# RWKV-7 heads in a decoder trunk: operands loaded once for two right sides, a chunk inverse kept in one orientation, and a row load moved behind the scan

## The reference, cut to what matters

```python
def step(state, inp):
    r_t, w_t, k_t, v_t, kk_t, a_t = inp
    sa = jnp.einsum('bhvk,bhk->bhv', state, -kk_t)
    state = (state * w_t[:, :, None, :] + sa[..., None] * (kk_t * a_t)[:, :, None, :]
             + v_t[..., None] * k_t[:, :, None, :])
    return state, jnp.einsum('bhvk,bhk->bhv', state, r_t)
```

## Time and profile before

| | us |
|---|---|
| median of 3 runs (lowest, highest) | 1743.28 (1740.84, 1746.19) |
| the profiled execution, its own time | 1744.99 |
| its span, first to last instruction | 1743.3 |
| PE busy | 1661.1 (95%) |
| DVE busy | 1001.9 (57%) |
| ACT busy | 738.5 (42%) |

### The profile page before, as it was taken

The page is one execution under the profiler, slowest core; times in us unless marked ns, Lnnn a source line. Parts: engine busy times, 40 slices in busy tenths (PEclk is TensorE's granted clock), DMA queues, the critical chain, the costliest instruction groups (busy, mean ns, idle before and its releaser), DMA issues.

```text
span 1743.3 us, 26994 instructions
## 1 busy us (share of the span) xinstructions
PE 1661.1 (95%) x11106; PEld 1385.8 (79%) x11106; DVE 1001.9 (57%) x1272; ACT 738.5 (42%) x985; POOL 144.2 (8%) x160
## 2 busy tenths in 40 slices
PE   7999998999899999999999989989999999999996
PEld 5777898888778888888877767878887788888885
DVE  3578564674675543434488974555657755434346
ACT  4535543363435232323267864624543542323231
POOL 6110110000000000000016630000000000000000
PEclk9999999999999999999999999999999999999998
DMA  5221002353133333333332320243521233333331
GB/s 198 73 74 37 4 4 99 133 152 105 35 102 93 99 95 99 95 99 119 97 121 73 97 73 25 83 130 101 159 85 40 94 109 97 97 97 97 97 121 61
DMA packets 41162, 159.75 MB, mean 92 GB/s; under 512 B 4560, under 2 KB 4688, under 8 KB 39632
## 3 DMA queue, kind: packets, MB, share of 16 engines
q1 hardware_dynamic: 40752, 155.93, 28.8%
q10 hardware_dynamic: 288, 2.10, 0.3%
HBM read 153.81 MB, written 4.19 MB: 91 GB/s over the span
## 4 chain that ended last, share of the span: by engine, by line
PE 79%; DVE 13%; ACT 4%; issue 2%; DMA 1%; POOL 1%; SPq 0%; DVEq 0%; ACTq 0%; POOLq 0%
PE bank L582 23%; PE bank L584 23%; PE bank L583 23%; DVE w_lo L1772 2%; DVE act_lo L1785 1%; DVE sconv L1788 1%; DVE h L1788 1%; ACT w_hi L1255 1%; DMA w_raw<-weights 1%; PE bank L763 1%; PE bank L1104 1%; DVE stage L2172 1%; DVE bank L1788 1%; PE bank L782 1%; PE bank L776 1%
## 5 line engine op out<-in xcount | busy, mean ns | idle before, releaser
L1772 DVE TENSOR_TENSOR w_lo<-w_raw,w_hi 128x1024 fp32r<-128x1024 f32 x263 | 325.8, 1240 | 313.5 <-ACT w_hi L1255 310.7
L582 PE MATMUL bank<-act_lo,w_hi 128*128 128x512 f32 x1048 | 417.2, 398 | 27.2 <-DVE w_lo L1772 16.0
L1255 ACT ACTIVATE w_hi<-w_raw 128x1024 fp32r<-128x1024 f32 x263 | 278.8, 1061 | 350.2 <-PE bank L584 336.3
L583 PE MATMUL bank<-act_hi,w_lo 128*128 128x512 f32 x1048 | 412.4, 394 | 0.0
L584 PE MATMUL bank<-act_hi,w_hi 128*128 128x512 f32 x1048 | 412.1, 393 | 0.0
L582 PEld LDWEIGHTS bank<-act_lo,w_hi 128*128 128x128 f32 x1048 | 199.3, 190 | 75.3 <-issue 17.3
L584 PEld LDWEIGHTS bank<-act_hi,w_hi 128*128 128x128 f32 x1048 | 199.2, 190 | 42.3
L583 PEld LDWEIGHTS bank<-act_hi,w_lo 128*128 128x128 f32 x1048 | 199.3, 190 | 41.7 <-issue 1.2
L582 PE MATMUL bank<-w_lo,aux_hi 128*128 128x512 f32 x576 | 224.9, 390 | 0.0
L583 PE MATMUL bank<-w_hi,aux_lo 128*128 128x512 f32 x576 | 224.4, 390 | 0.0
L584 PE MATMUL bank<-w_hi,aux_hi 128*128 128x512 f32 x576 | 224.4, 390 | 0.0
(11 more groups left out here) (362 smaller groups left out, 2058.6 us busy)
## 6 DMA issues: line engine op xcount, KB each, us to landing
w_raw<-weights SPq DMA_DIRECT2D x263, 512.0 KB, 3.6
gb<-ln_rows SPq DMA_DIRECT2D x6, 1024.0 KB, 7.2
stage<-x_feat SPq DMA_DIRECT2D x4, 512.0 KB, 6.2
h<-x_tok SPq DMA_DIRECT2D x1, 2048.0 KB, 7.7
stage<-mem_feat ACTq DMA_DIRECT2D x2, 1024.0 KB, 6.1
spill<-h SPq DMA_DIRECT2D x1, 2048.0 KB, 7.4
h<-spill SPq DMA_DIRECT2D x1, 2048.0 KB, 7.9
out<-h SPq DMA_DIRECT2D x4, 512.0 KB, 2.6
```

Source lines behind the costliest of these rows:

```text
L582: pe.matmul(o, whi, xlo, start=first, stop=False)
L583: pe.matmul(o, wlo, xhi, start=False, stop=False)
L1255: act.activation(w_hi[:, s], w_raw[:, s], ACT.Copy).then_inc(S("w_hi_done"), 1)
L1772: dve.tensor_tensor(w_lo[:, s], w_raw[:, s], f(w_hi[:, s]), ALU.subtract).then_inc(S("w_split"), 1)
```

## The change

1. `within_chunks` makes eight tiles from 64 products instead of ten from 160: each stationary operand (nbh, kh) is loaded once for 128 moving columns, 64 of rho and 64 of alpha, by an access pattern over two places (`both`). One DVE operation masks both halves and writes them to two places. The product alpha x nbh the other way round is gone.
2. The inverse is updated in one orientation: NBH for v below 5, XT_ for v = 5. After the first step and after each level below 5 DVE transposes the 32x32 blocks of the whole tile (`dve.transpose`, 128x1024). `level_z` makes one tile instead of two. The masks of a level stand for the other triangle.
3. `transitions(b, 0)` becomes `solved(b)`, `transitions(b, 1)` becomes `transitions(b)`: 32 products of 128 columns each instead of 64 of 64. ACT writes `rgt`, and DVE adds `rat`, to two places at a time.
4. The `rw` tiles move out of `within_chunks`: group 0 behind the bonus products, group 1 behind the LRU products. `bonus(1)` on DVE moves behind a convolution, `lru_scan` one level later with scans 2 and 3 behind the levels.
5. `lru_hi(0)` and `lru_hi(1)` on ACT move into the state loop, after states 3 and 6. The load of h moves behind chunk out0+5 and the end of the scan.

Cut to what is spoken of ("..." marks what is left out):

```diff
@@ sync
-                if c == FIRST["out0"] + 2:
-                    sp.wait_ge(S("rst_mm"), 1)
+                if c == FIRST["out0"] + 5:
+                    sp.wait_ge(S("ro_mm"), 2)
                     sp.dma_start(h[:], x_tok).then_inc(S("h_moved"), 16)
@@ helper
+        def both(rows, first, second, *inner):
+            one = mix[rows, (first - h_at) // 4:(first - h_at) // 4 + 1]
+            return bass.AP(one.tensor, one.offset, [one.ap[0], ((second - first) // 4, 2), *inner])
@@ tensor: within_chunks
-                for n, (lhs, rhs) in enumerate([(alpha, nbh), (nbh, alpha), (kh, alpha), (nbh, rho), (kh, rho)]):
...
+                for n, lhs in enumerate([nbh, kh]):
+                    for j in range(2):
+                        o = [take(f"rprod{b}", 4 * n + 2 * j + q) for q in range(2)]
+                        for m in range(NT):
+                            for q in range(2):
+                                feat = slice(RD * q, RD * q + RD)
+                                for c in (2 * m, 2 * m + 1):
+                                    right = both(feat, rho_at(b, j) + c * RC * 4, alpha_at(b, j) + c * RC * 4, (1, RC))
+                                    last = pe.matmul(o[q][rows_(c), m * P:m * P + P], lhs[feat, j, c * RC:c * RC + RC],
+                                                     right, start=True, stop=True)
@@ tensor: level_z
-                x_, y_ = NBH[b], yt_(b, v)
+                y_ = yt_(b, v)
                 pe.wait_ge(*out_sem(f"ryt{b}_{v}", 1))
-                if v < 5:
...
-                o = take(f"rz{b}_{v}", 1 if v < 5 else 0)
+                if v > 1:
+                    pe.wait_ge(S("r_xt"), 2 * (v - 2) + b + 1)
+                left, right = (XT_[b], y_) if v < 5 else (y_, XT_[b])
+                o = take(f"rz{b}_{v}", 0)
@@ tensor: solved
+                                    right = both(rows_(c), act_unit(7 + 4 * b, j) + at, alpha_at(b, j) + at, (1, RC))
+                                    last = pe.matmul(o[rows_(c), (2 * m + q) * P:(2 * m + q) * P + P],
+                                                     XT_[b][rows_(c), j, ct], right, start=True, stop=True)
@@ tensor: even_mixer
                 within_chunks(0)
                 bonus(1)
+                keys_times_values(0)
                 within_chunks(1)
                 lru()
+                keys_times_values(1)
@@ scalar
-            lru_hi(0)
-            lru_hi(1)
...
+                if c == 3:
+                    act.wait_ge(S("ro_tokens"), 2)
+                    lru_hi(0)
                 if c in (4, 5):
                     group_squares(c - 4)
+                if c == 6:
+                    lru_hi(1)
@@ vector
+                masks = m_two[:].unsqueeze(2).to_broadcast([P, 2, NT, RC])
+                for n in range(8):
...
+            def first_level(b):
                 for j in range(2):
...
+                    step(tt(three(XT_[b][:, j]), three(M_[b][:, j]), mid(m_lev[:, 0], NRC), MUL))
+                    step(tt(three(XT_[b][:, j]), three(XT_[b][:, j]), mid(eye2[:], NRC), ADD))
+                done(dve.transpose(NBH[b][:], XT_[b][:]), "r_x0")
 
             masked_products(0)
-            bonus(1)
+            first_level(0)
             for j in range(2, 4):
                 dve.wait_ge(S("in_out"), 15 + j)
                 convolution(j)
+                if j == 2:
+                    bonus(1)
             masked_products(1)
+            first_level(1)
...
+                done(tt(view, view, bank(f"rz{b}_{v}", 0)[:].rearrange("p (b n) -> p b n", n=n), ADD), "rz_out")
+                if v < 5:
+                    done(dve.transpose(XT_[b][:], NBH[b][:]), "r_xt")
...
-                    if b == 0 and v >= 3:
-                        lru_scan(v - 3)
+                    if b == 0 and v >= 4:
+                        lru_scan(v - 4)
+            lru_scan(2)
             lru_scan(3)
```

More of the change, by code:

```diff
@@ L468, in _ @@
             fill(m_lev[:], 1.0)
-            for v in range(6):
+            for q in range(2):
+                rows = slice(RC * q, RC * q + RC)
+                view = m_lev[rows, 0].rearrange("p (b u) -> p b u", u=2)
+                sel(view, ALU.is_equal, 0, [[-2, RC // 2], [0, 2]], 1, 0.0)
+                sel(view, ALU.is_ge, -1, [[0, RC // 2], [1, 2]], 0, 0.0)
+            for v in range(1, 6):
                 n = 1 << v
@@ new lines, in solved @@
+            def solved(b):
+                for j in range(2):
+                    for half in range(2):
+                        o = take(f"rgt{b}", 2 * j + half)
+                        for m in (0, 1):
+                            for q in range(2):
+                                for c in (4 * half + 2 * m, 4 * half + 2 * m + 1):
+                                    ct, at = cols_(c, q), cols_(c, q).start * 4
+                                    right = both(rows_(c), act_unit(7 + 4 * b, j) + at, alpha_at(b, j) + at, (1, RC))
+                                    last = pe.matmul(o[rows_(c), (2 * m + q) * P:(2 * m + q) * P + P],
+                                                     XT_[b][rows_(c), j, ct], right, start=True, stop=True)
+                        last.then_inc(S("mixer_mm"), 1)
@@ new lines, in transitions @@
+            def transitions(b):
+                pe.wait_ge(*out_sem(f"rgt{b}", 4))
+                for j in range(2):
+                    o = [take(f"rat{b}", 2 * j + s) for s in range(2)]
+                    for m in range(NT):
+                        for c in (2 * m, 2 * m + 1):
+                            s = c % 2
+                            for q in range(2):
+                                ct, at = cols_(c, q), cols_(c, q).start * 4
+                                right = both(rows_(c), h_at + (2 * b + j) * 2048 + at, act_unit(4 * b, j) + at, (1, RC))
+                                last = pe.matmul(o[s][RD * q:RD * q + RD, m * P:m * P + P], KH[b][rows_(c), j, ct], right,
+                                                 start=True, stop=True)
+                            if m == NT - 1:
+                                last.then_inc(S("mixer_mm"), 1)
@@ L1364, in _ @@
             tokens(0)
+            values_in(0)
             tokens(1)
```

198 lines of the change are left out of this document (72 added, 126 removed).

## The result

The changed kernel takes **1726.26 us** (median of four executions, 1725.62 to 1727.52), against 1743.15 (1740.84 to 1746.19) for the kernel before, run beside it: a ratio of 0.9897, 95% interval 0.9878 to 0.9917. It is faster by 17 us, where 21.8 were forecast, and lies inside the range of 1713 to 1733. The profiled execution took 1727.52 us, with a span of 1725.8.

What follows compares the result with a forecast made beforehand. PE was taken to bound levels and transitions, DVE the chunk products, something else the scan. Terms 5.4 + 13.6 + 2.8 + 4.1 - 1.0 - 0.6 - 2.5 = 21.8 us gave 1721.5 us against the median; range 1713 to 1733.

Steps and rivals of the forecast that it cites:

- chunk products: Chunk products, bound by DVE's masking: fewer DVE passes let the levels start at 190.3 instead of 195.7; gain 5.4 us.
- levels: Levels of the inverse: four product groups each time, 39.9 us instead of 53.5; gain 13.6 us.
- POOL's loss: Level 4: POOL's first pass over `dend` falls beside the LRU scan and stretches DVE; loss 1.0 us (0 to 2).
- transitions: `solved`, `even_output` and `transitions` with 128-column products: 14.8 us instead of 17.6; gain 2.8 us.
- scan: Scan: moving the load of h behind it removes an instruction stop and the low clock after it; gain 4.1 us.
- ACT's order: State loop on ACT: `lru_hi(1)` behind the last state copy pushes later ACT work and L911; loss 0.6 us.
- clock: One 3.4 us low-clock stretch in the chunk products, half a one behind level 4; loss 2.5 us (0 to 6).
- DVE would be the bound: Levels: rival with a transpose of 2.45 us, DVE work 9.3 us a level, 8.5 us lost, 1730; chance 0.17.
- Row tiles in one bank: `solved`: rival that row tiles writing one PSUM bank take turns at 128 columns, 7 us more, 1728; chance 0.07.
- The wait in level 5: Level 5's second group: PE waits 2.4 us because a scan stands between level 4's two adds on DVE.
- the stops that I had named: Chunk products: PE's stops at 169.4 to 175.2 (2 us busy of 6), allowed one low-clock stretch costing 1.7 us.
- the rival in which the clock falls and stays: Levels and transitions: PE at 1.2 GHz; kernel slower past 27 us of it, 1775 at the full 54; chance 0.05.

Runs made afterwards that it cites:

- scans last: Changed kernel with all four LRU scans on DVE behind the last level: 1718.61 us, ratio 0.9862; timed again 1720.23 us, ratio 0.9858.
- the third experiment: Changed kernel with POOL's two passes over dend started when the level 5 rz tiles are made, not the ryt tiles: 1726.95 us, ratio 0.9899.
- the filled wait: Changed kernel with four added useless 512-column products on PE just before it waits for level 5's second group: 1722.69 us, ratio 0.9876.
- the scans early: Changed kernel with the first LRU scan behind level 3 and the second behind level 4, as in the kernel before: 1731.9 us, ratio 0.9921.

## Why the prediction was right, and where it was off

The terms, from the first level to `L921`, in the profiled executions:

| term | forecast | measured | from |
|---|---|---|---|
| chunk products | 5.4 | 5.9 | levels start at 189.82, before 195.7; 0.6 of it is there before the stretch begins |
| levels, POOL's loss in it | 13.6 - 1.0 | 12.2 | 45.9 us to `solved`, less 4.6 for the clock, before 53.5 |
| transitions | 2.8 | 2.6 | 16.6 us, less 1.6 for the clock, before 17.6 |
| scan | 4.1 | 5.2 | 252.33 to 271.48 = 19.15, before 24.4 |
| ACT's order | -0.6 | -0.7 | 10.34 us, before 9.68 |
| clock | -2.5 | -6.3 | 1.5 + 3.1 + 1.6, below |
| sum | 21.8 | 18.9 | 18.75 by the `w_lo` starts at 301 us |

No run puts the second orientation or the separately loaded operands back: what the first three terms gained is read from the timelines, stretch against stretch.

- **The transpose** was taken at 1.25 us and takes 1.25; DVE's order in the first level (masks, adds, transposes, LRU) came out as laid down, and no level up to 4 waits. The Trainium skill's page "Vector Engine (DVE) Microarchitecture Reference", section 3.8, has one element per cycle and lane; by that the trace agrees (1.25 us against 1.23 for the subtraction of the same size). That DVE would be the bound, a chance of 0.17, was wrong for this transpose, and the doubled one shows how near it is: 1.25 us more per transpose brought waits and cost 13 us, nearly all of it by the low clock behind them.
- **Row tiles in one bank.** At full clock `solved` takes 7.20 us for its 64 products of 128 columns (scans last), 0.11 us each as forecast; the 64 of `transitions` take 3.72 us, 0.058 each. The two quarters write different halves of the partitions of one bank. The rule of the Trainium skill's page "TensorEngine Tiling (Array Packing)", section "Gotcha 1: PSUM Pressure", would have given 14 us for `solved`; by that rule the trace does not agree.
- **The wait in level 5.** Forecast were 2.4 us and 1.0 for POOL; 3.79 us came, of which 1.5 are POOL's, by the third experiment (2.27 without). Mechanism and place were right.
- **The load.** That the load makes TensorE stop, and that the clock follows, stands in both directions: put back it costs the scan 3.7 us, moved alone in the kernel before it takes 4.6 off it. That it is the supply of instructions that stops is my reading; the profile shows only that no releaser is there. The gain in the stretch was 1.1 us more than forecast: I had kept two waits for "issue" in the states (1.06 and 1.14), and only one is left, of 1.10.
- **The clock** is the term that was mis-sized: I had allowed one and a half stretches of 3.4 us, a loss of 2.5. The one in the chunk products (0.95 in the window) did not come behind the stops that I had named: those were there (1.86 and 1.60 us, up to 174.70) and brought none. It came at 157.1, at the end of a wait of 3.27 us for DVE that the forecast doesn't have, and since the levels start when forecast it cost nothing that can be seen. The one behind level 4 was not half a stretch but 13.7 us: the last two groups of level 5 took 3.41 + 6.83 us by their starts instead of 1.87 + 3.73, and `solved` 8.82 instead of 7.20, together 6.3 us. I had taken the length of such a stretch from the one in the rows, as if it were a constant of the chip. One of the signs that I had given for a wrong forecast, PE at 0.5 clock for long between 175 and 245 us, is therefore there, and the rival in which the clock falls and stays came true for a quarter of its stretch. That the pause causes it was only argued then, and is shown by the filled wait. It is partly luck that the total still lies well inside the range: 1.6 us more in the chunk products and the scan stand against 3.8 more lost to the clock.

The rest of the program gave 3.3 us more up to 1133 us and took 4.8 back by the end. Most of the latter is low clock in layer 1, in two stretches that the kernel before has in one execution and not in another, and whose length in the changed kernel is not explained. The medians put the change at 17 us in one set of runs and 19 in the other (0.9897, 0.9889).

The stretch of low clock in the levels is not set by the length of the pause. In all six traces that have one, the clock falls inside a pause, 0.6 to 3.7 us behind its start, and comes back only in `solved`, 2.7 to 5.2 us behind its first product. These windows reach from the first product of `solved` to that return, in the changed kernel, the one with POOL later, the one with the transposes twice and the one with the scans early; behind each the clock is at 1.00:

```profile
235.72:239.05 3.33, 3.33 (x36) 3.33 (x36) 3.19 (x5) 0.60 (x1) 0.00 (x0) 0.50 0.00 0
234.60:239.77 5.17, 5.17 (x54) 5.17 (x53) 5.03 (x5) 1.19 (x2) 1.99 (x1) 0.50 0.00 0
251.26:253.92 2.66, 2.66 (x31) 2.66 (x30) 2.56 (x4) 0.59 (x1) 0.00 (x0) 0.50 0.00 0
241.44:244.76 3.32, 3.32 (x37) 3.32 (x36) 3.18 (x5) 0.60 (x1) 0.00 (x0) 0.50 0.00 0
```

So the stretch is 13.7, 17.1, 51.2 or 27.3 us long mostly by how far ahead of `solved` the pause lies: behind the same wait of 2.27 us it is 17.1 us in level 5 and 27.3 in level 4. Outside the levels it is short: behind the first line here, in the chunk products, it is 3.4 us, and behind the second there is none.

```profile
157.38 4.36 PE L751 MATMUL bank<-ident,mix 128*128 128x128 f32 x24 [3.27 <-DVE mix L1804]
...
171.12 1.98 PE L741 MATMUL bank<-mix 64*64 64x128 f32 x64 [1.86 <-DVE mix L1804]
```

What stays open: why the clock does not come back during the levels, where TensorE is full (no run varies what it does there), why some pauses of 1.1 to 2.6 us bring it down and others do not, and what is behind the "issue" waits of 0.8 to 1.7 us in the states, which come with and without the load.

## What to carry to other kernels

When an edit shortens what bounds a stretch, list the waits that the engine gets in exchange, and price each at its length and at what the clock does behind it: here a wait of 3.8 us cost 10 in the trace, and its removal gave 7 to 8 us between the medians, 5 to 6 by the ratios. The price is highest where the work behind the pause lets the clock stay low. A side job (a scan, a pass of another engine over the same tiles) belongs behind the last thing that the bounding engine waits for, not between two of them; if a pause can't be avoided, cheap work in it can pay. A bulk load is not free because its own landing is hidden: among many short products of TensorE, 2 MB cost 3.7 to 4.6 us.

## What the hardware showed that was not expected

- In the levels the clock falls inside a pause of TensorE of 1.1 to 3.8 us, and then stays at 1.2 GHz (granted clock 0.50) for 13.7 to 51.2 us, with the engine full behind the pause, up to the products of `solved`. With four needless products in the pause the clock stays at 2.4 GHz.
- The length of a pause alone does not tell. In the changed kernel's chunk products 3.27 us are followed by 3.4 us of low clock, and 1.86 and 1.60 us by none; in the kernel with the scans last a wait of 2.55 us, at 322 us, is followed by none in one execution, and by 3.4 us in another.
- The low clock can hide what was made to be the bound: with it a level takes TensorE 13.7 us, and 9.4 us of VectorE's work no longer show.
- A pass of GpSimd over 1024 columns (1.90 to 2.28 us) stretches a VectorE product of 512 columns from 0.69 to 2.21 us. The product ends 0.55 us behind the end of GpSimd's pass, in the changed kernel (224.61 against 224.06) as in the rows of before (247.75 against 247.20), as if it had waited for the pass and not shared with it. Operations of the same size that read a bank beside such a pass keep their 0.69 us (229.24 in the changed kernel, 245.35 in the kernel before).
- The low clock comes and goes between executions of one program in the same place: 1.00 and 0.97 over 130 us, in executions of the kernel before of 1744.99 and 1749.07 us; and 13.7 and 17.1 us behind the same wait of 3.79 us, in two executions of the changed kernel.
